# Sigmoids, scan and exponentials of the decay placed one to two chunks later in the orders of ACT and VectorE of a recurrent layer

## The chip, the cores and the metric

One core of a Trainium2 chip runs one program. The metric is device time in microseconds (us) for one execution. TensorE is called PE, its weight load PEld, VectorE DVE, ScalarE ACT, GpSimd POOL and SyncE SP, as in the profile.

## What is computed

One inference step of a two-layer decoder trunk on a prompt of 512 tokens and 8 x 8 sampled tokens (576 columns in all), model width 1024, in 32-bit floats. Layer 0 mixes tokens by windowed attention, layer 1 by RWKV-7 time mixing; each is followed by a dense SwiGLU block, and every sub-layer ends in a layer norm. The part that matters here is the time mixing, in the reference's words cut to the decay and the state:

```python
w = -jax.nn.softplus(-(w0 + jnp.tanh(xw @ w1) @ w2)) - 0.5
a = jax.nn.sigmoid(a0 + (xa @ a1) @ a2)
kk = heads(k * k_k)
kk = kk / jnp.maximum(jnp.sqrt(jnp.sum(kk * kk, axis=-1, keepdims=True)), 1e-12)
decay = jnp.exp(-jnp.exp(heads(w)))
...
sa = jnp.einsum('bhvk,bhk->bhv', S, -kk_t)
S = (S * d_t[:, :, None, :] + sa[..., None] * (kk_t * a_t)[:, :, None, :]
     + v_t[..., None] * k_t[:, :, None, :])
```

The kernel uses that the logarithm of the decay is a constant times a sigmoid. It sums these logarithms along the tokens of a chunk with a scan, and takes exponentials of the sums.

## The kernel before, in words

The layout has features on the 128 partitions and tokens along the free axis. A dense product (helper `slab`, L657) splits both operands into a high and a low part and multiplies three times; these products, in all projections and in both SwiGLU blocks, fill most of the time and come before and after the stretch of interest.

**The recurrent layer** works on *units*. Unit 0 holds the sampled tokens of all heads; units 1 to 8 are the eight pairs of heads for the prompt (512 tokens, one pair on the 128 partitions). The prompt is cut into 8 *chunks* of 64 tokens. The loop over `SLOTS` = 12 *slots* overlaps several units. In slot s these run together:

- A1, unit i = s (slots 0 to 8): sigmoids, decay, normed keys, and the scaled operands for the unit.
- A2, unit a = s - 1: the inverse of a small triangular matrix, level by level (`level_y`, `level_x`), token-major copies of b, k and v, and the masked Gram matrices.
- SB, sampled pair j = s - 2, and C, the group norm and gate of pair g = s - 4.
- B, pair q = s - 3 (slots 3 to 10): the state chain over the 8 chunks, the only part that is serial over chunks.

The state chain of one chunk c goes: PE `chain_u` (L1012, L1016), DVE copies the result into `uc` (L2074), PE `chain_sa` (L1026), ACT copies into `sac` (L1600), PE `chain_s` (L1037), DVE updates the state `S_c` (L2082, L2085). The next chunk starts from `S_c`. ACT also scales the last state into `spc` (L1593) ahead of each chunk.

**What sets the order.** Each engine has a list written out by hand: `for s in range(SLOTS)`, `for c in range(NCH)`, and in each chunk c branches that put the other work of the slot between the links of the chain. The three lists are in `slot` for PE, in ACT's loop at L1667 and in DVE's loop at L2141. POOL has a plain list for each slot: the level masks, the sample masks, the scaled gate (L588), the scaled r (L594), then the scaled keys (L609). SP moves the sampled state in and out. Semaphores carry every dependence between the lists.

**The functions that the edit places.**

- `sigmoids(i)` on ACT waits for `lora2(i)` of PE (L860 and L861, in chunk 0 after `chain_s`), then writes the sigmoid of the decay's logits into `cc` (L1501) and the sigmoid for a into `sga` (L1504). In slots 1 to 8 it is preceded by a load of ACT's function table.
- `cumulated(i)` on DVE waits for the first of these and runs the scan over `cc` in place (L1993).
- `decays(i)` on ACT asks for the other function table (L1515), waits for the scan, and writes two exponentials (L1521 into `e2`, L1522 into `e0`).

Their readers: `kk_sum` on PE (L873, chunk 2 after `chain_s`) waits for the first sigmoid; `kk_floor` on DVE (L2000, chunk 2) follows it; `kk_root` on ACT (a logarithm L1530 and an exponential L1532) stands in chunk 3 ahead of `chain_sa`; `scaled_z` on DVE (chunk 4) reads `e0`; POOL's scaled gate and scaled r read `e2` and `e0`, and `scaled_b` (chunk 5) and `bonus_terms` (chunk 7) on DVE read what POOL wrote. `dev_squares(g)`, a square of 512 columns (L1640), stands in ACT's chunk 2.

In the kernel before, ACT runs `sigmoids` in chunk 0 after its token-major copy of b, and `decays` in chunk 1 after the copy of k. DVE runs `cumulated` at the end of chunk 0, after the state update `chain_s` and so ahead of the `uc` copy of chunk 1.

Of the kernel before, what the change touches and what calls it, by code (L numbers as in the profile page):

```python
# [137 lines left out]
def build_program(nc, ins, outs, scratch):  # L138
    cols, width = constant_layout()
    ctx = ExitStack()  # L140
    with ctx:
# [137 lines left out]
        def psb(b):  # L279

            return ps[:, b, :]
# [1004 lines left out]
        def _(act):  # L1286
# [209 lines left out]
            def sigmoids(i):  # L1496

                act.wait_ge(ev("wkv_zero"), 1)
                act.wait_ge(ev("lora2_mm"), i + 1)
                if i:  # L1500
                    A(padded[:, :, 1:], chunks(psb(G1)), ACT.Sigmoid, bias=col(R_W0, i - 1)).then_inc(ev("sig_w"), 1)  # L1501
                    act.wait_ge(ev("ga"), i)
                    act.wait_ge(ev("f"), i)
                    A(sga[:], psb(G2), ACT.Sigmoid, bias=col(R_A0, i - 1)).then_inc(ev("sig_a"), 1)  # L1504
                    return
                for j in range(NPAIR):
                    out = A(padded_s[:, j, :, 1:], ps[:, G1, tk(j)].rearrange("p (b t) -> p b t", t=DT), ACT.Sigmoid, bias=col(R_W0, j))
                out.then_inc(ev("sig_w"), 1)
                for j in range(NPAIR):
                    out = A(sga[:, tk(j)], ps[:, G2, tk(j)], ACT.Sigmoid, bias=col(R_A0, j))  # L1510
                out.then_inc(ev("sig_a"), 1)

            def decays(i):

                nc.scalar.preload_act_table_set("natural_log_exp_and_others")  # L1515
                act.wait_ge(ev("scan"), i + 1)
                if i:
                    act.wait_ge(ev("kt"), i)
                    act.wait_ge(ev("zt"), i)
                    act.wait_ge(ev("rt"), i)  # L1520
                    A(chunks(e2[:]), padded[:, :, 1:], ACT.Exp, scale=KAPPA).then_inc(ev("e2"), 1)  # L1521
                    A(e0[:, 0:PADP], cc[:], ACT.Exp, scale=-KAPPA).then_inc(ev("e0"), 1)  # L1522
                else:
                    A(sequences(e2[:]), padded_s[:, :, :, 1:], ACT.Exp, scale=KAPPA).then_inc(ev("e2"), 1)
                    A(e0[:], cc_s[:], ACT.Exp, scale=-KAPPA).then_inc(ev("e0"), 1)
# [141 lines left out]
            for s in range(SLOTS):  # L1667
                i, a, j, q, g = s, s - 1, s - 2, s - 3, s - 4
                A1, A2, SB, B, C = i < UNITS, 0 <= a < UNITS, 0 <= j < NPAIR, 0 <= q < NPAIR, 0 <= g < NPAIR
                CSM = s == SLOTS - 2  # L1670
                whole = A2 and a >= 1
                if C:
                    last_state(g)
                    outputs(g)
                if A1:
                    kk_squares(i)
                for c in range(NCH):
                    if B and c >= 1:
                        scaled_state(q, c)
                    if c == 0 and whole:  # L1680
                        corner(a)
                    elif c == 1 and A2:
                        level_y(a, 1)
                    elif c == 2:
                        if C:
                            dev_squares(g)
                        if CSM:
                            dev_squares_s()
                    elif c == 3 and A1:
                        kk_root(i)  # L1690
                    elif c == 4 and SB:
                        sample_state(j)
                    elif c == 5 and whole:
                        level_y(a, 4)
                    elif c == 6 and A1:
                        key_mix(i)
                    elif c == 7:
                        if whole:
                            merge_t(a)
                    if B:  # L1700
                        chain_sa(q, c)
                    if c == 0:
                        if A2:
                            token_major(a, 0, "tb", "tok_b")
                        if A1:
                            sigmoids(i)
                    elif c == 1:
                        if A2:
                            token_major(a, 1, "tkk", "tok_k")
                        if A1:  # L1710
                            decays(i)
                    elif c == 2 and A2:
                        level_y(a, 2)
                    elif c == 3:
                        if A2:
                            token_major(a, 2, "tv", "tok_v")
                        if whole:
                            level_y(a, 3)
                        if CSM:
                            gn_root_s()  # L1720
                    elif c == 4 and C:
                        gn_root(g)
                    elif c == 5 and A1:
                        chunk_decays(i)
                    elif c == 6:
                        if SB:
                            sample_sa(j)
                        if whole:
                            merge_y(a)
                    elif c == 7:  # L1730
                        if A2:
                            inverse_blocks(a)
                        if C:
                            operand_high(g)
                        if SB:
                            sample_update(j)
                        if CSM:
                            act.wait_ge(ev("normed_step"), normed_at("z_s"))
                            A(zh[:, :, SEQ:T], chunks(outs_s[:]), ACT.Copy).then_inc(ev("normed_step"), 1)
# [23 lines left out]
        def _(dve):  # L1763
# [377 lines left out]
            for s in range(SLOTS):  # L2141
                i, a, j, q, g = s, s - 1, s - 2, s - 3, s - 4
                A1, A2, SB, B, C = i < UNITS, 0 <= a < UNITS, 0 <= j < NPAIR, 0 <= q < NPAIR, 0 <= g < NPAIR
                CSM = s == SLOTS - 2
                whole = A2 and a >= 1
                for c in range(NCH):
                    if B:
                        chain_u(q, c)
                    if c == 0 and A2:
                        level_first(a)  # L2150
                    elif c == 3 and A2:
                        level_x(a, 2)
                    elif c == 4:
                        if A1:
                            scaled_z(i)
                        if whole:
                            level_x(a, 3)
                        if CSM:
                            hat_s()
                    elif c == 5:  # L2160
                        if A1:
                            scaled_b(i)
                        if SB:
                            sample_ut(j)
                        if C:
                            bonus(g)
                        if CSM:
                            bonus_s()
                    elif c == 6:
                        if SB:  # L2170
                            sample_u(j)
                        if A1:
                            mixed_keys(i)
                    elif c == 7:
                        if SB:
                            sample_out(j)
                        if A1:
                            bonus_terms(i)
                    if B:
                        chain_s(q, c)  # L2180
                    if c == 0 and A1:
                        cumulated(i)
                    elif c == 1 and A2:
                        level_x(a, 1)
                    elif c == 2 and A1:
                        kk_floor(i)
                    elif c == 3 and A1:
                        unit_keys(i)
                    elif c == 4 and C:
                        hat(g)  # L2190
                    elif c == 5 and whole:
                        level_x(a, 4)
                    elif c == 6:
                        if C:
                            gated(g)
                        if A2:
                            masked_gram(a, 0, G1, "br", "incl")
                    elif c == 7:
                        if A2:
                            masked_gram(a, 2, G2, "kz", "strict")  # L2200
                            masked_gram(a, 1, G1, "kr", "incl")
                        if CSM:
                            gated_s()
# [39 lines left out]
```

## Time and profile before

| what | value |
|---|---|
| median of 3 runs | 2028.53 us (2024.49 to 2029.5) |
| profiled execution, its own time | 2028.29 us |
| span of the profiled execution, first to last instruction | 2026.5 us |
| PE busy | 1748.2 us (86%), 20270 matmuls |
| DVE, ACT, POOL busy | 679.6, 683.4, 613.4 us |
| mean granted PE clock | 0.914 of full speed |
| slots 3 to 8, from the first `uc` copy of slot 3 | 1106.3 to 1380.4 us |
| slot 9 | 1380.4 to 1422.9 us |

How to read it: "busy" counts the time in which an engine executed instructions; matmuls are pipelined, so their busy time is modelled. Times of a timeline are us from the start of the span. A row of the timeline has the start, the duration, the engine, the line of the kernel, the operation, output<-inputs, the shape and how many instructions were merged; in brackets is the idle time of the engine just before, and who ended it. A row of a group has the line, the engine, the count, then busy us and mean ns of one, then the idle time before and what ended it. In a row of busy times by stretch stand the stretch, its length, the busy time of PE, PEld, DVE, ACT and POOL with the number of their instructions, the mean granted clock of PE (1.00 is full speed), the share of the DMA engines and GB/s. "issue" is time in which an engine waited for nothing that the profile shows. The chunks of a slot are told apart by the `uc` copies of DVE (L2074), one in each.

### The profile page before, as it was taken

The page shows a single profiled execution, that of the slowest core. Times are in us where ns is not written, and L with a number is a line of the kernel's source. Part 1 is how long each engine was busy: PE and PEld are TensorE (multiplying, and loading weights), DVE is VectorE, ACT ScalarE, POOL GpSimd, SP SyncE. Part 2 cuts the span into 40 slices and gives each one's busy share as a digit, 9 for nine tenths or more (in the row PEclk, how much of TensorE's full clock was granted, in tenths as well). Part 3 has the DMA queues.
Part 4 walks back from the last instruction along what each step waited for, and adds up shares of the span by engine and source line. Part 5 has one row for each costly group of instructions (what it writes and reads, how often), then busy time and mean ns, then how long its engine had stood idle before and what let it go on. Part 6 is the DMA issues. An engine that isn't in the chain of part 4 may idle for free.

```text
span 2026.5 us, 46453 instructions
## 1 busy us (share of the span) xinstructions
PE 1748.2 (86%) x20270; PEld 1578.7 (78%) x20270; DVE 679.6 (34%) x942; ACT 683.4 (34%) x1118; POOL 613.4 (30%) x316
## 2 busy tenths in 40 slices
PE   4989696999998993888967888888885999998994
PEld 4965495999998993877936766666575999998994
DVE  2136246222222226233034344443246222222224
ACT  3135214433331112232235454443234433332112
POOL 3313123433333332222214222221033333333331
PEclk8969787999999997899978899999788999999997
DMA  7410012222222221312110000000041222222221
GB/s 214 113 36 1 21 52 70 84 83 83 83 83 75 82 82 66 105 46 72 42 24 14 14 15 15 15 15 10 12 126 42 80 79 81 82 83 82 85 71 47
DMA packets 236247, 125.93 MB, mean 62 GB/s; under 512 B 49275, under 2 KB 233196, under 8 KB 235956
## 3 DMA queue, kind: packets, MB, share of 16 engines
q1 hardware_dynamic: 227330, 108.97, 19.2%
q10 hardware_dynamic: 8786, 14.98, 2.3%
q8 instruction: 110, 1.80, 0.4%
q14 instruction: 21, 0.17, 0.0%
HBM read 116.33 MB, written 12.64 MB: 64 GB/s over the span
## 4 chain that ended last, share of the span: by engine, by line
PE 69%; issue 15%; DVE 8%; POOL 4%; ACT 3%; ACTq 1%; POOLq 0%; DVEq 0%
PE ps L657 51%; POOL wl L522 2%; PE ps L751 1%; PE ps L946 1%; PE ps L827 1%; PE ps L936 1%; PE ps L1026 1%; PE ps L776 1%; DVE xl L1968 1%; DVE x L1817 1%; PE ps L1037 1%; POOL x L537 1%; DVE mf L1962 1%; PE ps L915 1%; PE ps L1016 1%
## 5 line engine op out<-in xcount | busy, mean ns | idle before, releaser
L522 POOL TENSOR_TENSOR wl<-raw,wh 128x1024 fp32r<-128x1024 f32 (+1 forms) x172 | 451.3, 2625 | 878.2 <-ACT wh L1294 878.2
L657 PE MATMUL ps<-xh,wh 128*128 128x288 f32 x2112 | 460.8, 300 | 92.2 <-DVE xl L1968 40.0
L1294 ACT CAST wh<-raw 128x1024 fp32r<-128x1024 f32 (+1 forms) x172 | 190.3, 1108 | 843.4 <-PE ps L657 843.4
L657 PE MATMUL ps<-xl,wh 128*128 128x288 f32 x2112 | 457.4, 299 | 0.0
L657 PE MATMUL ps<-xh,wl 128*128 128x288 f32 x2112 | 456.8, 298 | 0.0
L657 PEld LDWEIGHTS ps<-xh,wh 128*128 128x128 f32 x2112 | 344.7, 191 | 99.1 <-issue 82.2
L657 PEld LDWEIGHTS ps<-xl,wh 128*128 128x128 f32 x2112 | 345.8, 192 | 0.0
L657 PEld LDWEIGHTS ps<-xh,wl 128*128 128x128 f32 x2112 | 345.3, 191 | 0.0
L1843 DVE TENSOR_TENSOR lnw<-lnw,ps 128x576 f32<-128x576 f32 x44 | 33.2, 754 | 390.2 <-PE ps L657 373.1
L657 PE MATMUL ps<-hh,wh 128*128 128x288 f32 x704 | 151.4, 297 | 11.3 <-DVE hl L1848 11.3
L657 PE MATMUL ps<-hl,wh 128*128 128x288 f32 x704 | 151.0, 296 | 0.0
L657 PE MATMUL ps<-hh,wl 128*128 128x288 f32 x704 | 150.9, 296 | 0.0
L657 PEld LDWEIGHTS ps<-hh,wh 128*128 128x128 f32 x704 | 114.3, 191 | 11.7 <-POOL wl L522 11.7
L657 PEld LDWEIGHTS ps<-hl,wh 128*128 128x128 f32 x704 | 114.2, 190 | 0.0
L657 PEld LDWEIGHTS ps<-hh,wl 128*128 128x128 f32 x704 | 114.0, 190 | 0.0
L1848 DVE TENSOR_TENSOR hl<-lnw,hh 128x576 f32 x44 | 97.0, 2205 | 46.2 <-ACT hh L1338 46.2
L1789 DVE TENSOR_TENSOR x<-x,ps 128x576 f32 x32 | 24.1, 755 | 256.5 <-PE ps L657 256.5
L1794 DVE TENSOR_TENSOR lnw<-lnw 128x576 f32<-128x576 f32 x32 | 80.6, 2520 | 3.9 <-ACT lnw L1321 3.5
L603 POOL TENSOR_TENSOR zl<-oS,zh 128x512 fp32r<-128x512 f32 x8 | 10.1, 1267 | 205.7 <-ACT zh L1652 205.7
L1956 DVE SCALAR_TENSOR_TENSOR mt<-xx,prm,x 128x576 f32<-128x576 f32 x24 | 23.7, 992 | 98.0 <-PE ps L657 97.3
L827 PE MATMUL ps<-mf,lnw 128*64 128x288 f32 (+2 forms) x128 | 42.3, 467 | 14.7 <-DVE mf L1962 14.4
L2085 DVE SCALAR_TENSOR_TENSOR S_c<-ps,pc,spc 128x64 f32<-128x64 f32 x56 | 15.6, 279 | 106.5 <-PE ps L1037 104.5
(340 smaller groups left out, 2320.8 us busy)
## 6 DMA issues: line engine op xcount, KB each, us to landing
raw<-in_ffn_w_gu SPq DMA_DIRECT2D x88, 512.0 KB, 3.8
raw<-in_ffn_w_down SPq DMA_DIRECT2D x32, 704.0 KB, 4.6
raw<-in_rwkv_w_rkv SPq DMA_DIRECT2D x24, 512.0 KB, 4.1
raw<-in_attn_w_qkv SPq DMA_DIRECT2D x24, 256.0 KB, 3.7
raw<-in_attn_w_o SPq DMA_DIRECT2D x32, 128.0 KB, 3.0
raw<-in_rwkv_w_o SPq DMA_DIRECT2D x8, 512.0 KB, 4.3
spread<-table ACTq DMA_DIRECT2D x1, 3072.0 KB, 15.5
x_kept<-x ACTq DMA_DIRECT2D x1, 2304.0 KB, 8.2
```

The source lines that it names most:

```text
L522: nc.gpsimd.tensor_tensor(wl[:, s, 0:ph.kb, :], raw[:, s, 0:ph.kb, :], wh[:, s, 0:ph.kb, :].bitcast(F32), ALU.subtract).then_inc(raw_free, 1)
L537: nc.gpsimd.tensor_tensor(x[:, j, :], x[:, j, :], lnw[:, 0, :], ALU.subtract).then_inc(ev("ln_sub"), 1)
L657: out = mm(ps[:, 2 * a + b, 0:TH], w[:, s, k, :], o[:, k0 + k, t0:t0 + TH], start=(first and k == 0 and w is wh and o is high), stop=(last ...
L751: out = mm(ps[:, 2 * (t % 2) + i // 2, (i % 2) * W:(i % 2 + 1) * W], qkvT[part, G * GROUP + i, qb * WIN:(qb + 1) * WIN], qkvT[part, KB + G ...
L776: out = mm(ps[part, 6 + pair % 2, :], vtok[:, qb - nkb + 1 + kb, g * HD:(g + 1) * HD], PT[:, u % 2, kb * 512:(kb + 1) * 512], start=(kb == ...
L827: out = mm(ps[part, bank + b, 0:TH], w(k), mf[:, k % 2, t0:t0 + TH], start=(k == 0), stop=(k == KB - 1))
L1294: nc.scalar.copy(wh[:, s, 0:ph.kb, :], raw[:, s, 0:ph.kb, :]).then_inc(hi_done, 1)
L1789: V.tensor_tensor(blk, blk, acc(a), ALU.add).then_inc(acc_free, 1)
L1794: V.tensor_tensor(squares, squares, lnw[:, 3:4, :], ALU.add).then_inc(ev("ln_acc"), 1)
L1843: V.tensor_tensor(hbuf[:, q, :].rearrange("p (h n) -> p h n", h=2), gbuf[:, q, :].rearrange("p (h n) -> p h n", h=2), acc(2 * q + 1), ALU.mult
L1848: V.tensor_tensor(hl[:, bass.ds(2 * i + q, 1), :], hbuf[:, q:q + 1, :], hh[:, bass.ds(2 * i + q, 1), :].bitcast(F32), ALU.subtract).then_i ...
L1956: V.scalar_tensor_tensor(mt[:, j % 2, :], xx[:, j, :], col(R_MIX + operand[1], j), x[:, j, :], ALU.mult, ALU.add).then_inc(ev("mt"), 1)
```

## The change

It moves three calls in two lists. On ACT `sigmoids(i)` goes from chunk 0 to chunk 1, after the token-major copy of k, and `decays(i)` from chunk 1 to chunk 2, after `level_y(a, 2)`. On DVE `cumulated(i)` goes from the end of chunk 0 to chunk 2, between the `uc` copy and the state update. The lists of PE, POOL and SP, all operands and all semaphores stay.

```diff
                     if c == 0:
                         if A2:
                             token_major(a, 0, "tb", "tok_b")
-                        if A1:
-                            sigmoids(i)
                     elif c == 1:
                         if A2:
                             token_major(a, 1, "tkk", "tok_k")
                         if A1:
+                            sigmoids(i)
+                    elif c == 2:
+                        if A2:
+                            level_y(a, 2)
+                        if A1:
                             decays(i)
-                    elif c == 2 and A2:
-                        level_y(a, 2)
...
                     if c == 0 and A2:
                         level_first(a)
+                    elif c == 2 and A1:
+                        cumulated(i)
                     elif c == 3 and A2:
...
                     if B:
                         chain_s(q, c)
-                    if c == 0 and A1:
-                        cumulated(i)
-                    elif c == 1 and A2:
+                    if c == 1 and A2:
                         level_x(a, 1)
```

## Rows read from the trace of the kernel before

**Rows 1.** The page, part 4: the chain that ended last, by engine, share of the span.

```profile
PE 69%; issue 15%; DVE 8%; POOL 4%; ACT 3%; ACTq 1%; POOLq 0%; DVEq 0%
```

**Rows 2.** Busy us: slots 3-8, 7, 9, chunk 1: PE, PEld, DVE, ACT, POOL, PEclk.

```profile
1106.30:1380.40 274.10, 234.44 (x7535) 183.16 (x7536) 113.44 (x266) 132.98 (x306) 68.16 (x65) 0.93 0.08 16
...
1290.80:1335.40 44.60, 38.53 (x1268) 29.53 (x1270) 19.26 (x46) 22.68 (x53) 12.03 (x11) 0.96 0.08 16
...
1380.40:1422.90 42.50, 36.98 (x1251) 28.43 (x1250) 14.14 (x38) 15.37 (x42) 7.47 (x8) 0.96 0.05 11
...
1298.70:1303.60 4.90, 4.67 (x130) 4.25 (x130) 1.23 (x5) 2.42 (x4) 0.89 (x1) 0.68 0.02 3
```

**Rows 3.** Groups by line in slots 3 to 8.

```profile
L1026 PE MATMUL ps<-uc,tt 64*64 64x64 f32 x192 | 17.0, 255 | 19.8 <-DVE uc L2074 19.1 <-issue 0.2
...
L915 PE MATMUL ps<-cst,kx 64*64 64x64 f32 x192 | 11.2, 305 | 0.0
...
L1993 DVE TENSOR_TENSOR_SCAN cc<-reset,cc 128x520 f32<-128x520 f32 x6 | 8.8, 1465 | 19.9 <-ACT cc L1501 19.9
...
L1501 ACT ACT_TABLE_LOAD x6 | 7.7, 1283 | 9.8 <-PE ps L861 9.8
...
L873 PE MATMUL ps<-sq,cst 128*128 128x512 f32 x12 | 6.8, 645 | 0.0
...
L861 PE MATMUL ps<-twa,wa 64*128 64x512 f32 x12 | 6.7, 641 | 0.0
```

**Rows 4.** Timeline of slot 7, chunk 0 to the copy of chunk 1.

```profile
1290.80 0.23 DVE L2074 COPY uc<-ps 128x64 f32<-128x64 f32 x1 [1.05 <-PE ps L1012]
...
1295.15 0.33 PE L1016 MATMUL ps<-S_c,zr 64*64 64x64 f32 x4
...
1295.31 1.28 ACT L1501 ACT_TABLE_LOAD   x1 [1.40 <-PE ps L861]
...
1297.19 0.68 ACT L1504 ACTIVATE sga<-ps,prm 128x512 f32<-128x512 f32 x1
...
1298.68 0.19 DVE L2074 COPY uc<-ps 128x64 f32<-128x64 f32 x1
```

**Rows 5.** Timeline of slot 9, chunk 1.

```profile
1384.05 0.33 PE L1016 MATMUL ps<-S_c,zr 64*64 64x64 f32 x4 [0.25 <-DVE S_c L2082]
...
1384.43 0.23 DVE L2074 COPY uc<-ps 128x64 f32<-128x64 f32 x1 [0.43 <-PE ps L1016]
...
1386.54 0.60 ACT L1558 ACTIVATE tok<-ps 128x512 f32<-128x512 f32 x1 [0.82 <-PE ps L915]
...
1386.89 0.45 PE L946 MATMUL ps<-xt,yb 32*32 32x32 f32 x32
```

**Rows 6.** Timeline of slot 7, chunks 1 to 3.

```profile
1301.99 1.28 ACT L1515 ACT_TABLE_LOAD   x1
...
1302.00 0.75 PE L946 MATMUL ps<-xt,yb 32*32 32x32 f32 x64
...
1303.82 0.62 ACT L1522 ACTIVATE e<-cc 128x520 f32<-128x520 f32 x1
...
1305.06 0.21 ACT L1600 ACTIVATE sac<-ps 128x64 f32<-128x64 f32 x1
...
1305.29 0.38 ACT L1563 ACTIVATE yb<-ps 128x256 f32<-128x256 f32 x1
...
1307.82 0.63 ACT L1530 ACTIVATE sq<-sq 128x512 f32<-128x512 f32 x1 [1.45 <-DVE sq L2000]
...
1309.02 0.21 ACT L1600 ACTIVATE sac<-ps 128x64 f32<-128x64 f32 x1
```

**Rows 7.** PE in slot 9, chunk 3, and the instruction queue in slots 3 to 8.

```profile
1396.25 0.33 PE L1047 MATMUL ps<-gr,tok 64*64 64x64 f32 x3 [1.06 <-issue]
...
q8 instruction: 59, 0.97, 1.5%
```

**Rows 8.** Timeline of ACT in slot 1: the key norms' logarithm.

```profile
1066.66 0.63 ACT L1530 ACTIVATE sq<-sq 128x512 f32<-128x512 f32 x1 [1.23 <-DVE sq L2000]
```

## The prediction

> **What bounds the kernel now.** I read the page first: over the whole execution PE holds 69% of the chain that ended last and waiting without a shown cause ("issue") 15% [rows 1]. That average is mostly dense products, which the edit doesn't touch. The edit lies in the recurrent layer's slots, so I read busy time by stretch. Six slots (3 to 8) both run the state chain of one head pair (B) and start the next unit (A1): 274.1 us, 45.7 each, with PE busy 234.4 [rows 2]. Slot 9 runs the chain but starts no unit: 42.5 us.
>
> Inside a slot the chain alternates PE, DVE, PE, ACT, PE, DVE in each chunk, and each engine takes its list in order. So an instruction that waits on ACT or DVE holds up the chain link listed behind it. The groups of the six slots show where: the scan of the decays (L1993) left DVE idle 19.9 us before it, waiting for the sigmoid of ACT, and runs 1.465 us each; PE then sat 19.1 us for DVE's `uc` copy in front of L1026; ACT's table load before the sigmoid waited 9.8 us for L861 [rows 3]. That is 3.3 us of DVE waiting and about 2.7 us of PE idling once a slot. The timeline of slot 7 shows the order: the chain's next product L1016 is done by about 1295.5, yet its copy starts at 1298.68, because ACT first loads the table (1295.31), computes both sigmoids (until 1297.87), and DVE scans [rows 4]. Slot 9, without these, starts that copy 0.38 us after L1016 starts (1384.05 to 1384.43) [rows 5]. What limits chunk 0 is thus the ACT sigmoid plus the scan, and not PE.
>
> A second cost follows the idle. In the 4.90 us of chunk 1 of slot 7 the granted clock was 0.68 of full speed, the slot's mean is 0.96 [rows 2]: PE had idled and then ran partly at 1.2 instead of 2.4 GHz. The token transposes L915 took 11.2 us of PE in six slots, 305 ns a matmul [rows 3].
>
> **The change part by part.** No instruction is added or removed: the same two sigmoids, two table loads, two exponentials and one scan a slot, no DMA, and nothing moves in the lists of PE, POOL or SP. I work it out in slot 7. Times in us of the trace.
>
> 1. *Sigmoids and scan leave chunk 0.* DVE copies `uc` for chunk 1 at 1295.15 + 0.38 = 1295.53 instead of 1298.68: 3.15 earlier [rows 4, 5].
>
> 2. *Chunk 1 without the idle.* In slot 9 L946 starts 2.46 after the `uc` copy (1384.43 to 1386.89) [rows 5]; in slot 7 it takes 3.32 (1298.68 to 1302.00) [rows 4, 6]. I take slot 9's: another 0.86, so L946 at 1297.99, 4.0 earlier. Bounds: 0 if PE stays at the low level, 0.86 if it doesn't; I take the latter, since the idle that comes before the low clock is what goes.
>
> 3. *Sigmoids in chunk 1.* ACT evicts the token-major keys at +2.11 after the copy (1386.54) for 0.60, so it is free at 1298.24 [rows 5]. The block of load and two sigmoids is 1295.31 to 1297.87, 2.56 [rows 4], and ends at 1300.80. Today the end of the exponentials (1304.44) is followed by `sac` of chunk 2 at 1305.06, 0.62 later [rows 6]; so `sac` comes at 1301.42. That is 3.64 earlier: 0.36 of the gain is given back, the rest of the block runs beside PE's and DVE's level step and `uc` copy. The scan, now set between chunk 2's `uc` copy and its L2085 in DVE's list, starts at about 1300.25, when the first sigmoid is done, and with 1.465 [rows 3] ends at 1301.7. L2085 needs `sac`, which ends at 1301.64, and a PE product after it, so the scan is just covered.
>
> 4. *Exponentials in chunk 2.* After `sac` ACT copies one level (1305.29, 0.38) [rows 6]; by the same offsets it is free at 1302.03. Load and two exponentials are 1301.99 to 1304.44, 2.45, and end at 1304.48. The root's logarithm L1530 could start at `sac` + 2.76 = 1304.18 (1305.06 to 1307.82 today) and waits until about 1304.7, past one small copy; with the 1.20 from it to the next `sac` [rows 6] this `sac` is at 1305.9, against 1309.02: 3.1 earlier. From there on the lists are as before.
>
> 5. *Who waits for the exponentials.* POOL's scaled gate and scaled r start when they are done and are read by DVE only in chunks 5 and 7; DVE's scaled z, in chunk 4, is the first reader of all. The exponentials end in chunk 2, so one chunk (4.9 us in slot 7 [rows 2]) or more covers them; were that cover gone, up to 2.45 a slot would show.
>
> A rule speaks against steps 3 and 4. Slot 7's load starts at 1301.99 and its last exponential ends 2.45 later, the load itself being 1283 ns in all the slots [rows 3, 6]. The Trainium skill (ScalarE: Activation LUTs, "What ACT_TABLE_LOAD costs") adds a drain of about 1380 ns to each load, some 2.66 us for a switch. By that each moved block would be 1.38 longer and a slot would gain about 0.3 us, an estimate by that page; the trace shows no room for the drain, and I go by the trace.
>
> 6. *Slots 1 and 2* have no state chain; there the key norms depend on ACT. ACT idles 1.23 before the logarithm [rows 8]; a block of 2.45 set before it can cost 0 to 1.2 in each. I take 0.5: 1.0 together. Slot 0 runs one unit alone, in the same dependence order: nothing.
>
> 7. *What comes late next: PE's instructions.* A denser PE shows stalls that waiting hid. In slot 9 PE stood 1.06 in the middle of L1047, cause "issue", and the six slots fetched 59 packets, 0.97 MB, of instructions [rows 7]. Bounds per slot: 0, and 1.06. Stalls in chunks 1 and 2 fall under the ACT blocks; for chunk 3 on I take half, 0.5.
>
> The Trainium skill (Runtime: NRT & Kernel Launch, "Instruction fetch mechanics") says that instructions come in blocks of 16 KiB and that the cost is mostly hidden. By that item 7 would be nothing, and the time would be 2010.7, an estimate by that page.
>
> Sum: 6 x (3.1 - 0.5) = 15.6, less 1.0, is 14.6 us. The profiled execution took 2028.29 us (1.8 more than its span), 0.2 under the median of the runs, 2028.53, so the sum needs no correction: 2028.3 - 14.6 = 2013.7.
>
> **The rivals.** About 0.3% (6 us) is what a measurement of this kernel can tell from no change.
>
> *A, as summed* (0.72): 11 to 21 us faster. 21 is six times 3.5, with no stall and a little more of the low clock gone.
>
> *B, PE's own supply is the bound* (0.16). For it: slot 9, free of all that moves here, still took 42.5, and the matmuls that it lacks are L873, 1.1 us of PE a slot (6.8 in six), and the pair L860 and L861, which overlap, 1.1 more (6.7) [rows 3]; with them it would take 44.7, against 45.7 on average [rows 2]. Against it: slot 9's stalls beyond slot 7's lie partly where ACT now sets the pace. It gives 6 x 1.0 = 6 us: 2022.3, at the edge of what can be told.
>
> *C, the blocks are given back in full, slower* (0.05). Place: ACT between `sac` of chunk 1 and `sac` of chunk 3. If neither block finds time in which ACT idles, the chain pays 2.56 + 2.45 = 5.0 a slot against the 4.0 won in chunks 0 and 1; with slots 1 and 2 at their 1.2 each that is 6 x 1.0 + 2.4 = 8.4 slower: 2036.7. It decides once more than 4.0 of the 5.0 shows. Against it: ACT is busy only 2.42 of the 4.90 us of chunk 1 [rows 2].
>
> *D, chunk 0 isn't freed* (0.05). The PE link L1016 stands behind L861 and the copy behind it; if PE, not the scan, set that copy, nothing would move: 2028 or so. Against it: L1016 starts 3.5 before the copy [rows 4].
>
> *E, more than 21 us* (0.02), by the low clock vanishing from other chunks too.
>
> The range is A's with half of B's reach: 2007.5 to 2021.5. Faster by over 0.3% is A, E and two thirds of B, 0.84; within 0.3% the rest of B and D, 0.11; slower C, 0.05.
>
> **What would show it.** Right: the wait of L1993 falls from 19.9 to under 3 us over the slots, the one of L1026 from 19.1 to a few; the `uc` copy of chunk 1 comes 4.7 us after that of chunk 0 instead of 7.9; L915 nears 218 ns as other transposes; slots of about 43; the seconds before `sac` in chunks 2 and 3 go to ACT. Wrong: equal gaps from chunk 0 to 1, PE stalls by "issue" growing by 2 us a slot (B), a wait of L2085 for the scan or of PE for `sac` of chunk 3 by over 2 us (C), or a time that changes in the dense products, where nothing was edited.

## The result and the profile after

The changed kernel took 2008.25 us (median of 4 runs, 2000.65 to 2011.49) beside 2029.01 us for the kernel before (median of 4, 2024.49 to 2035.79). The ratio is 0.989, 95% interval 0.9848 to 0.9931. On the prediction's base of 2028.53 us that is 2028.53 x 0.989 = 2006.2 us, just under the low end of the range (2007.5), where 2013.7 was forecast. The direction was right, the gain half as large again as forecast. A second, longer measurement of the same file gave 2009.34 against 2027.71 us, 0.9906 [0.9874, 0.9938]; on the same base that is 2009.5 us, inside the range. So the size of the miss is between 4 and 6 us, and the stretches below say where it lies.

The page of the kernel after: its span and instruction count, busy times, and the chain that ended last by engine (part 4).

```profile
span 1998.9 us, 46453 instructions
...
PE 1729.4 (87%) x20270; PEld 1565.8 (78%) x20270; DVE 679.6 (34%) x942; ACT 682.3 (34%) x1118; POOL 610.1 (31%) x316
...
PE 68%; issue 15%; DVE 8%; ACT 4%; POOL 4%; ACTq 1%; POOLq 0%; DVEq 0%
```

It hardly differs from [rows 1]: the edit is too small to be seen in averages. The stretches show it. Here are slots 3 to 8, slot 7, and chunk 1 of slot 7, in the columns of [rows 2] (length, then busy us of PE, PEld, DVE, ACT, POOL, the granted clock, DMA share, GB/s).

```profile
1102.20:1353.80 251.60, 223.71 (x7535) 172.86 (x7535) 112.64 (x266) 131.18 (x306) 65.44 (x65) 0.99 0.08 17
1270.00:1312.40 42.40, 37.91 (x1266) 28.54 (x1269) 19.12 (x45) 22.54 (x53) 11.11 (x11) 1.00 0.09 18
1274.80:1279.40 4.60, 4.27 (x196) 3.67 (x194) 1.28 (x5) 2.98 (x6) 3.11 (x4) 1.00 0.04 9
```

The six slots went from 274.1 to 251.6 us, and two things make up the 22.5. PE's busy time fell by 10.7 us (234.4 to 223.7) with the same matmuls, since the mean clock rose from 0.93 to 0.99. PE's idle time fell by 11.8 (39.7 to 27.9). The difference of the two profiled executions, 2028.29 - 2000.65 = 27.6 us, is larger than either median says. Of it 7.2 lie in the attention stage (from its first matmul, L730, to its last, L810: 145.2 to 138.0 us), where nothing was edited; over the fourteen profiles of this study that stage took 138.0 to 145.5. So slots are compared with slots here, and whole times only by medians.

The groups of slots 3 to 8, in the columns of [rows 3]: busy, mean ns of one | idle before, releaser.

```profile
L1026 PE MATMUL ps<-uc,tt 64*64 64x64 f32 x192 | 15.9, 243 | 3.6 <-DVE uc L2075 3.2
L1501 ACT ACT_TABLE_LOAD x6 | 7.7, 1283 | 0.1
L1994 DVE TENSOR_TENSOR_SCAN cc<-reset,cc 128x520 f32<-128x520 f32 x6 | 7.4, 1241 | 2.2 <-ACT cc L1501 2.2
L915 PE MATMUL ps<-cst,kx 64*64 64x64 f32 x192 | 6.8, 218 | 0.2 <-issue 0.2
```

PE's wait for the `uc` copy fell from 19.1 to 3.2 us, the scan's wait for the sigmoid from 19.9 to 2.2, the sigmoid's load now starts without a wait, and L915 runs at 218 ns instead of 305. The scan itself takes 1.24 us instead of 1.47. The timeline of slot 7, which answers to [rows 4] and [rows 6]:

```profile
1274.39 0.33 PE L1016 MATMUL ps<-S_c,zr 64*64 64x64 f32 x4
...
1274.77 0.23 DVE L2075 COPY uc<-ps 128x64 f32<-128x64 f32 x1 [1.17 <-PE ps L1016]
...
1277.50 1.28 ACT L1501 ACT_TABLE_LOAD   x1
...
1279.38 0.68 ACT L1504 ACTIVATE sga<-ps,prm 128x512 f32<-128x512 f32 x1
...
1279.51 1.24 DVE L1994 TENSOR_TENSOR_SCAN cc<-reset,cc 128x520 f32<-128x520 f32 x1
...
1280.66 0.23 ACT L1600 ACTIVATE sac<-ps 128x64 f32<-128x64 f32 x1
...
1281.56 0.32 PE L936 MATMUL ps<-xs,lm 32*32 32x32 f32 x14 [0.66 <-issue]
...
1281.94 0.38 ACT L1563 ACTIVATE yb<-ps 128x256 f32<-128x256 f32 x1 [1.04 <-PE ps L936]
...
1282.34 1.28 ACT L1515 ACT_TABLE_LOAD   x1
...
1284.17 0.62 ACT L1522 ACTIVATE e<-cc 128x520 f32<-128x520 f32 x1
...
1284.94 0.61 ACT L1530 ACTIVATE sq<-sq 128x512 f32<-128x512 f32 x1
...
1286.12 0.20 ACT L1600 ACTIVATE sac<-ps 128x64 f32<-128x64 f32 x1
```

Slot 7 begins at 1270.04, so the copy of chunk 1 (1274.77) comes 4.73 us into the slot; it was 7.88 [rows 4]. The copy starts 0.38 after L1016, as in slot 9. The scan now runs between the `uc` copy and the state update of chunk 2, and each `sac` follows the ACT block set before it. The level step L936 stops for 0.66 us in the middle, and ACT's next copy (L1563) waits for it.

### The profile page after: what moved, and what is told of

Its sections match the earlier page's. It is cut to its first block, busy times and chain, and to the rows that moved or that the text cites. A ratio compares the mean times of both kernels' runs of the same rounds, so it can differ in the third digit from the quotient of the medians.

```text
span 1998.9 us, 46453 instructions
## 1 busy us (share of the span) xinstructions
PE 1729.4 (87%) x20270; PEld 1565.8 (78%) x20270; DVE 679.6 (34%) x942; ACT 682.3 (34%) x1118; POOL 610.1 (31%) x316
## 4 chain that ended last, share of the span: by engine, by line
PE 68%; issue 15%; DVE 8%; ACT 4%; POOL 4%; ACTq 1%; POOLq 0%; DVEq 0%
PE ps L657 52%; POOL wl L522 3%; PE ps L936 1%; PE ps L827 1%; PE ps L946 1%; DVE xl L1969 1%; PE ps L1026 1%; DVE x L1818 1%; PE ps L776 1%; ACT S L1403 1%; POOL x L537 1%; DVE mf L1963 1%; PE ps L751 1%; PE ps L1037 1%; DVE S L1892 1%
## 5 line engine op out<-in xcount | busy, mean ns | idle before, releaser
L537 POOL TENSOR_TENSOR x<-x,lnw 128x576 f32<-128x576 f32 x16 | 30.3, 1924 | 63.6 <-DVE lnw L1811 63.6
```

Of the source, the lines that this page charges most:

```text
L537: nc.gpsimd.tensor_tensor(x[:, j, :], x[:, j, :], lnw[:, 0, :], ALU.subtract).then_inc(ev("ln_sub"), 1)
```

## The experiments

The theory T is the prediction's mechanism, resized after the result: the scan and what it waits for keep the `uc` copy of chunk 1 back by 3.15 us a slot; that idle time of PE brings the low clock behind it; both go. The rivals of each run are in its expectation. The table is the yardstick: length of slots 3 to 8 (from `uc` copy to `uc` copy), mean length of chunks 0 to 3 in them and the sum of chunks 4 to 7, then the us that PE ran at the lower clock level (1.2 GHz) by the trace's clock records, PE's "issue" waits with their count, and PE busy, all within those slots. For the fourteen profiles, in us:

| kernel | slots 3-8 | c0 | c1 | c2 | c3 | c4-7 | low clock | issue | PE busy |
|---|---|---|---|---|---|---|---|---|---|
| before | 274.0 | 8.39 | 5.10 | 4.23 | 3.64 | 24.31 | 41.0 | 6.6, 10 | 234.3 |
| before again (e9) | 273.1 | 8.40 | 5.02 | 3.96 | 3.81 | 24.32 | 34.1 | 8.5, 13 | 232.3 |
| after | 251.6 | 5.22 | 4.26 | 4.55 | 4.09 | 23.83 | 6.8 | 8.9, 15 | 223.7 |
| after again (e1) | 252.0 | 5.20 | 4.33 | 4.58 | 3.92 | 23.98 | 6.8 | 9.1, 15 | 223.9 |
| e2 scan only | 254.5 | 5.28 | 5.25 | 4.03 | 3.87 | 23.98 | 3.4 | 11.1, 15 | 221.1 |
| e3 blocks in chunk 1 | 267.5 | 5.23 | 4.24 | 7.41 | 3.90 | 23.83 | 27.3 | 6.7, 10 | 229.1 |
| e4 exponentials only | 271.3 | 8.39 | 4.46 | 4.34 | 4.02 | 24.02 | 30.7 | 6.1, 10 | 230.6 |
| e5 late from slot 3 | 252.8 | 5.20 | 4.59 | 4.50 | 4.07 | 23.76 | 3.4 | 10.6, 17 | 222.9 |
| e6 idle put back | 279.5 | 9.41 | 5.06 | 4.45 | 3.98 | 23.68 | 37.5 | 6.2, 9 | 233.0 |
| e7 blocks left out | 254.9 | 5.19 | 4.51 | 4.20 | 3.82 | 24.77 | 17.1 | 12.1, 15 | 226.0 |
| e8 root behind link | 257.0 | 5.21 | 4.59 | 4.63 | 3.71 | 24.69 | 13.7 | 14.2, 19 | 225.0 |
| e10 smaller idle | 253.6 | 6.71 | 3.68 | 4.40 | 3.81 | 23.67 | 6.8 | 5.4, 8 | 222.1 |
| e11 stream +128 | 257.6 | 4.75 | 4.54 | 4.65 | 4.09 | 24.91 | 23.9 | 9.9, 17 | 229.8 |
| e12 stream +64 | 259.9 | 5.73 | 4.57 | 4.55 | 4.12 | 24.37 | 17.1 | 13.4, 20 | 228.1 |

### e1: the changed kernel again

No edit.

> The changed kernel once more, with five rounds. The theory (T) has three parts: the scan's wait ahead of the uc copy was 3.1 us in each of slots 3 to 8, PE's low clock after that idle cost 0.9 more in chunk 1 and about as much again in other chunks, and the two ACT blocks give back 0.8 a slot; slots 0 to 2 lose 2.9. By T the six slots again take 251 to 254 us (before: 274.1) and the time falls by 18 to 23 us. Rival L (luck of the profiled run): the low clock outside chunk 1 comes back, the six slots take 256 to 260 us, and the time falls by 14 to 17 us.

Measured 2009.34 us, 0.9906 [0.9874, 0.9938]. The windows row of slots 3 to 8:

```profile
1106.30:1358.30 252.00, 223.87 (x7536) 172.38 (x7538) 112.59 (x266) 131.17 (x306) 65.42 (x65) 0.99 0.08 17
```

Both figures of T hold (251 to 254 us, 18 to 23 us less). The six slots repeat within 0.4 us, so their gain is no accident of one profile.

### e9: the kernel before again

No edit; one run, 2034.34 us.

> The kernel before once more, for a second profile of it. T: chunk 0 takes 7.9 to 8.9 us in all six slots, L915 about 300 ns a matmul, slots 3 to 8 take 270 to 275 us. Of the first profile's 6.0 us for chunk 6 of slot 3, where others have 3.9, T says nothing; if it is 3.9 here, 2 us of the profiled gain of slots 3 to 8 are chance. Rival: the six slots repeat at 274 within 0.5 us and all of the 22.4 us gained belong to the change.

```profile
1108.60:1381.70 273.10, 232.26 (x7531) 181.65 (x7533) 113.15 (x266) 132.72 (x306) 68.18 (x65) 0.94 0.08 16
```

The slots repeat within 1 us, as T asks; so does the 6.0 us of chunk 6 of slot 3. Slots 0 to 2 do not: 72.13 us here, 69.45 in the first profile of the same file. That matters for e5.

### e2: only the scan moves

```diff
+                    elif c == 1 and A1:
+                        cumulated(i)
...
-                    if c == 0 and A1:
-                        cumulated(i)
-                    elif c == 1 and A2:
+                    if c == 1 and A2:
```

Against the kernel before. ACT's list stays as it was, with sigmoids in chunk 0 and exponentials in chunk 1.

> Of the three moves only the scan is moved, to chunk 1 of DVE behind the uc copy; sigmoids and exponentials stay in chunks 0 and 1. T: the uc copy of chunk 1 comes 4.7 us after that of chunk 0, as in the changed kernel, sac of chunk 1 waits about 1 us for the sigmoids, and nothing stands in chunk 2, so that a slot gains 2.8 us plus the clock, against 3.1 plus the clock: six slots 252 to 257 us, slots 0 to 2 at their old length, time 15 to 21 us less. Rival S (the sigmoids' place is what counts, since ACT serves the chain): the chain only moves its wait from DVE to ACT and the six slots take 264 us or more.

Measured 2013.42 us, 0.991 [0.9877, 0.9944], 14.3 less than before where T wanted 15 to 21; the slots are inside T's 252 to 257. Two groups of slots 3 to 8, and PE's wait for `sac` there (sum, count, longest):

```profile
L1993 DVE TENSOR_TENSOR_SCAN cc<-reset,cc 128x520 f32<-128x520 f32 x6 | 8.4, 1393 | 9.4 <-ACT cc L1501 9.4
L915 PE MATMUL ps<-cst,kx 64*64 64x64 f32 x192 | 6.8, 218 | 0.2 <-issue 0.2
```

```profile
PE ps L1037 <- ACT sac L1600: 6.7, 12, 1.0
```

The scan alone brings the slots to 254.5, 19.1 us under the mean of the two profiles of before (273.6), of the 21.8 that the whole change brings (to 251.8). The low clock is gone. What the moved ACT blocks add is in chunk 1: 5.25 against 4.3, since the `sac` of chunk 1 behind the sigmoids is late by up to 1.0 us; of the 1.0 us a slot, chunk 2 gives 0.5 back and chunk 3 0.1.

### e4: only the exponentials move

```diff
+                    elif c == 2:
+                        if A2:
+                            level_y(a, 2)
                         if A1:
                             decays(i)
-                    elif c == 2 and A2:
-                        level_y(a, 2)
```

Against the kernel before: the exponentials go to chunk 2, the sigmoids and the scan stay. The sigmoids alone were not moved in any run.

> Of the three moves only the exponentials are moved, to chunk 2; sigmoids and scan stay in chunk 0. T: chunk 0 keeps its 7.9 to 8.9 us, sac of chunk 2 comes 0.6 earlier and the logarithm of chunk 3 waits for the block, so a slot changes by less than 0.5 us: six slots 272 to 277 us, time within 0.3% of before. Rival: the exponentials' block in chunk 1 was a cost by itself; without it the six slots fall below 270 us.

Measured 2029.91 us, 1.0 [0.9979, 1.0022]; PE's wait for `uc` in slots 3 to 8:

```profile
PE ps L1026 <- DVE uc L2075: 19.2, 12, 3.0
```

The wait is the old one (19.1). Chunk 1 is shorter by 0.6, chunks 2 and 3 longer by 0.54 together. The six slots took 271.3 us, 2.3 under before and 0.7 under T's range; 2.1 of that is chunk 6 of slot 3, which took 3.89 us here and 6.01 in both profiles of before. By itself this move is worth nothing that can be measured.

### e3: both blocks in chunk 1

```diff
                             sigmoids(i)
-                    elif c == 2:
-                        if A2:
-                            level_y(a, 2)
-                        if A1:
                             decays(i)
+                    elif c == 2 and A2:
+                        level_y(a, 2)
```

Against the changed kernel: ACT's copy into `sac` for chunk 2 now stands behind both blocks.

> The changed kernel with the exponentials back in chunk 1, right behind the sigmoids; the scan stays in chunk 2. T: both ACT blocks and the scan between them stand ahead of sac of chunk 2, which comes 2.2 us later than in the changed kernel; nothing stands in chunk 2 after it (0.5 back): a slot is 1.6 us longer, six slots 260 to 263 us, time 9 to 13 us less than before. Rival S2 (ACT blocks are covered wherever they stand): as the changed kernel, 251 to 254 us.

Measured 2022.05 us, 0.9977 [0.9955, 0.9999], 5.7 less than before where T gave 9 to 13. PE's wait for `sac` in slots 3 to 8, and slot 7's timeline:

```profile
PE ps L1037 <- ACT sac L1600: 16.4, 11, 2.9
```

```profile
1291.51 0.62 ACT L1522 ACTIVATE e<-cc 128x520 f32<-128x520 f32 x1
...
1293.02 0.48 PE L1037 MATMUL ps<-sac,tok 64*64 64x64 f32 x4 [2.28 <-ACT sac L1600]
...
1294.06 2.07 PE L873 MATMUL ps<-sq,cst 128*128 128x512 f32 x2
```

PE stands 2.28 us for `sac`, and what follows runs at the lower clock level (granted 0.50 from 1293.0 to 1296.4): L873 takes 2.07 for its two matmuls where six such pairs took 6.8 before [rows 3], 1.13 each. ACT never waited for the scan; it went from block to block without a pause, so it is the length of the two blocks that keeps `sac` back. Chunk 2 grows by 2.8 us, and 15.7 of the 21.8 us are gone (251.8 to 267.5), more than the 8 to 11 that T gave it. T had counted the wait and not the clock behind it. So the place of the exponentials does matter, if the sigmoids are moved too: it is both blocks ahead of one `sac` that cost.

### e6 and e10: idle time put back

```diff
-                    if c == 1 and A2:
+                    if c == 0 and A1 and B:
+                        for _ in range(6):
+                            link(V.tensor_tensor(l0[:], l0[:], l0[:], ALU.max))
+                    elif c == 1 and A2:
```

Against the changed kernel: DVE does six (e10: three) extra operations of no effect (the larger of a tile and itself) where the scan stood, so PE idles though ACT's order is the new one.

> The changed kernel with six short vector operations on a tile of DVE alone (about 2.8 us together) at the end of chunk 0 in slots 3 to 8: the idle of PE is back, and nothing else of the old order. T: a slot pays those 2.8 us, 0.9 for the low clock in chunk 1, L915 rises from 218 to about 300 ns a matmul, and low clock shows in other chunks too, so 3.5 to 4.5 us a slot: six slots 273 to 279 us, or as before. Rival F: the clock has no part in it and a slot pays 2.8 or less, six slots 268.5 us or less, L915 at 218 ns.

> As the run with the idle put back, with three of the six vector operations: they took 5.9 us together there, so about 2.9 here. T: chunk 0 is about 1.3 us longer than in the changed kernel (the operations begin at 5.0 us after the slot's first uc copy less 1.5, and the copy of chunk 1 could have come at 4.7), PE idles some 1 us, and the low clock doesn't return: six slots 258 to 262 us, low clock under 15 us, L915 near 218 ns. Rival: any idle in chunk 0 brings the low clock; L915 again near 290 ns and six slots over 263 us.

Measured 2038.78 us, 1.0061 [1.0037, 1.0086] for e6, and 2012.55, 0.9909 [0.9878, 0.994] for e10. The groups of e6, then of e10, in slots 3 to 8:

```profile
L2186 DVE TENSOR_TENSOR l<-l 128x256 f32<-128x256 f32 x36 | 33.2, 923 | 1.0
L1026 PE MATMUL ps<-uc,tt 64*64 64x64 f32 x192 | 16.9, 255 | 25.1 <-DVE uc L2075 24.6
L915 PE MATMUL ps<-cst,kx 64*64 64x64 f32 x192 | 10.5, 292 | 0.0
```

```profile
L2186 DVE TENSOR_TENSOR l<-l 128x256 f32<-128x256 f32 x18 | 17.9, 992 | 0.4
L1026 PE MATMUL ps<-uc,tt 64*64 64x64 f32 x192 | 15.8, 241 | 9.6 <-DVE uc L2075 9.1
L915 PE MATMUL ps<-cst,kx 64*64 64x64 f32 x192 | 6.6, 218 | 0.0
```

In e6 PE waits 24.6 us for the copy, about 4.1 a slot (21.8 of the 24.6 in chunk 1); L915 is back at 292 ns, PE's busy time at 233.0, and 37.5 us run at the low level. So idle time alone, with the scan and the sigmoids elsewhere, brings the low clock back. The operations took 923 ns, about twice what was set for them, so the wait overshot the old one and the slots with it: 279.5 us, 5.9 over before and 0.5 over T's 273 to 279. In e10 the wait is 9.1 us, 1.5 a slot, and the low clock stays away: 6.8 us, as without any wait. Here T failed: it wanted 258 to 262 us and 253.6 came. 1.5 us more in chunk 0 of each slot cost only 1.8 in all six instead of 6 to 10, as chunk 1 shrank by 0.6 to 3.68 and the later chunks by another 0.6 together. The last 1.5 us by which the copy comes earlier are worth little. That PE has work of its own list left at that point, done meanwhile in e10 and later otherwise, would explain it; no run takes that apart.

### e5: slots 0 to 2 in the old order

```diff
+                        if A1 and not B:
+                            sigmoids(i)
...
-                        if A1:
+                        if A1 and B:
...
-                    elif c == 2 and A1:
+                    elif c == 2 and A1 and B:
...
+                    if c == 0 and A1 and not B:
+                        cumulated(i)
```

Against the changed kernel (cut; the exponentials go likewise): the new places only where a state chain runs.

> The new places in the slots that run the state chain (3 to 8), the old places in slots 0 to 2. T: slots 0 to 2 return to their 69.4 us from kk_squares of unit 0 to the first uc copy (72.3 in the changed kernel), the six slots stay at 251 to 254; the time is 2 to 3 us under the changed kernel. Rival: the 2.9 us of slots 0 to 2 were the clock's chance, and their length stays within 1 us of 72.3.

Measured 2010.07 us, 0.9915 [0.9885, 0.9944]. Slots 0 to 2 took 69.63 us against 72.3 (after), as T asks. But e9 took 72.13 and e8, with the old order there too, 71.96. So the old order gave about 69.5 twice and about 72 twice; the five profiles with the changed kernel's order there (after, e1, e6, e7, e10) all lie between 72.0 and 72.4. The means differ by 1.3 us, the profiles of one order by 2.7, so a loss may be there, but neither its size nor the 2.9 us that T read from one pair of profiles is shown. The six slots stayed (252.8), and the time is no better than that of the changed kernel, where T wanted 2 to 3 us.

### e7: the blocks left out

```diff
+                if i >= 3:
+                    A(cc[:, 0:1], psb(G1)[:, 0:1], ACT.Copy).then_inc(ev("sig_w"), 1)
+                    ...
+                    A(sga[:, 0:1], psb(G2)[:, 0:1], ACT.Copy).then_inc(ev("sig_a"), 1)
+                    return
```

Against the changed kernel. From unit 3 on this leaves out the sigmoids of decay and a, the exponentials and their table loads, and puts one-column copies in their place.

> The changed kernel without the sigmoids of the decay and of a, the exponentials and the table loads in units 3 to 8 (copies of one column take their places); this part of the computation is left out. T: what the two blocks still cost in chunks 2 and 3 (0.8 us a slot) is gained, 4 to 6 us over the six slots, which take 246 to 248 us. Rival P (PE's supply of instructions is the bound): waits of PE with the cause issue grow as the others shrink, and the six slots stay at 250 us or more.

Measured 2009.1 us, 0.9907 [0.9876, 0.9939]: no better than with them. Some of PE's waits in slots 3 to 8, sum, count, longest:

```profile
PE ps L936 <- issue: 2.7, 4, 0.8
...
PE ps L1057 <- issue: 2.5, 3, 1.1
```

T wanted 246 to 248 us; 254.9 came. ACT's 25 us less busy time (131.2 to 105.7) shorten chunk 2 by 0.37 and chunk 3 by 0.2, and chunks 4 to 7 pay 0.9 for it, with "issue" waits of 12.1 us instead of 9, and 17.1 us of low clock, all of it in chunks 5 and 6. The kernel without these blocks is no faster, so what ACT still costs in the changed kernel isn't to be had by unloading ACT alone.

### e8: a wait less for `sac` of chunk 3

```diff
-                    elif c == 3 and A1:
+                    elif c == 3 and A1 and not B:
...
+                        if A1 and B:
+                            kk_root(i)
```

e5 with the logarithm of the key norms behind the `sac` of chunk 3 instead of before it (cut; DVE's use of it goes to chunk 4).

> As e5, and in slots 3 to 8 the key norms' logarithm and exponential come behind sac of chunk 3 instead of ahead of it, with the unit keys on DVE behind the uc copy of chunk 4. T: sac of chunk 3 comes up to 1.2 us earlier and no link waits instead, so a slot gains 0.5 to 1.2 us against e5: six slots 245 to 250 us. Rival: the unit keys and scaled z, now together in chunk 4, or PE's stalls take it back: six slots within 2 us of e5.

Measured 2015.44 us, 0.9924 [0.9897, 0.9951]. T missed again: it wanted 245 to 250 us for the six slots and 257.0 came, 4.2 over e5 and so beyond the rival's 2 as well. Chunk 3 went from 4.07 to 3.71, as planned, and chunks 4 to 7 from 23.76 to 24.69. Waits of PE in the slots:

```profile
PE ps L936 <- issue: 4.0, 5, 1.0
...
PE ps L946 <- issue: 2.8, 4, 1.3
...
PE ps L1057 <- issue: 2.1, 3, 1.0
```

Issue waits are at 14.2 us, the most of all runs, and the low clock at 13.7 (3.4 in e5). Two edits that take work or a wait off ACT both end in more issue waits and more low clock; which of the two costs the time isn't taken apart.

### e11 and e12: the instruction stream moved

```diff
+            for _ in range(256):
+                pe.wait_ge(ev("proj_taken"), 1)
             ident2 = const("ident2")
```

Against the changed kernel: waits on an event long passed, before the layer, shift all later instructions of PE in their stream. Two such waits make one instruction, so 256 of them are 128 instructions (e12: 128 waits, 64 instructions).

> The changed kernel with 128 more wait instructions in PE's list ahead of slot 0, each satisfied at once: every later instruction of PE lies 128 places further in its stream. Theory Q (PE's short stops with the cause issue sit where a block of the stream ends, so they move with the stream): inside slots 3 to 8 the stops are at other places, 1.4 to 2.2 us later or earlier in each slot, their sum is between 6 and 13 us, and the slots' length changes by up to 3 us either way. Rival: they belong to certain instructions and stay where they are in both profiles of the changed kernel (3.2 to 3.4 us into slot 4 at L906, 4.0 into slot 5 at L1041, about 11.3 into slots 7 and 8 at L936).

> As the one before with 64 instructions. Q: the stops move by about half as far, and the length of slots 3 to 8 lies anywhere within 3 us of 252. Rival: they stay.

In both profiles of the changed kernel PE stops in the middle of a group of matmuls mostly at the same places, for instance L906 in slot 4 (0.97 and 1.08 us) and L936 in slot 8 (0.93 and 0.89); some differ, as L936 in slot 3 (0.67 and 0.15). The first fence is slot 4 of the changed kernel; then the stop in front of L867, behind the waits, and one in slot 4 of e11; then one in slot 6 of e12.

```profile
1145.22 0.39 PE L906 MATMUL ps<-cst,bt 64*64 64x64 f32 x6 [0.97 <-issue]
```

```profile
1042.51 0.44 PE L867 MATMUL ps<-twa,wa 64*128 64x64 f32 x1 [15.45 <-issue]
...
1171.22 1.12 PE L875 MATMUL ps<-sq,cst 128*128 128x512 f32 x2 [1.56 <-issue]
```

```profile
1244.40 0.68 PE L908 MATMUL ps<-cst,bt 64*64 64x64 f32 x16 [2.06 <-issue]
```

The stops move with the stream, and the traces show what ends them. The DMA queue that brings instructions (q8) lands 59 packets in these six slots in every profile. Over the fourteen profiles PE has 193 issue waits there, and each of the 193 ends 1.18 to 1.71 us after such a packet has landed. That stretch behind the packets is about an eighth of the time, and of PE's 481 other waits about 7% end in it. So these stops are PE waiting for its own instructions and not for data. The six slots took 257.6 and 259.9 us, 6 to 8 more than before the shift, which was beyond the 3 us expected. PE's busy time rose by 6.0 and 4.3 us of this, with more low clock (23.9 and 17.1 us). The waits themselves cost much: slots 0 to 2 grew by 14.7 and 7 us, so the whole times say nothing of the shift, 2029.7 us, 1.0018 [0.9996, 1.004], and 2027.01, 0.9994 [0.9977, 1.001].

## Why the prediction was right or wrong

By its own steps, from means of two profiles each (before and e9; after and e1), per slot:

**Steps 1 and 2** were right. Chunk 0 fell by 3.18 us (3.15 forecast), chunk 1 by 0.77 (0.86). The copy comes 4.73 us into slot 7, as forecast. e2 shows that it is the scan's move that did it, and e6 that the low clock in chunk 1 comes from the idle time. e10 shows a limit: of the 3.15 us in chunk 0 the last 1.5 bring only 0.3 a slot.

**Steps 3 and 4** were right on the mean. Chunks 2 and 3 grew by 0.75 together, 0.9 forecast. In slot 7, where the working was done, `sac` of chunk 2 comes 10.62 us into the slot, as forecast, but `sac` of chunk 3 at 16.08 instead of 15.1, since the stop of 0.66 us in L936 keeps back ACT's copy and the block behind it. The wait for `sac` is 2.9 us in all and nowhere above 0.4:

```profile
PE ps L1037 <- ACT sac L1600: 2.9, 11, 0.4
```

The rule of the Trainium skill (ScalarE: Activation LUTs, "What ACT_TABLE_LOAD costs") on a drain for each load was rightly set aside: load, two activations and no gap between them, 1282.34 to 1284.79, again 2.45 us. e3 shows what keeps these steps cheap: both blocks before one `sac` cost 15.7 us.

**Step 5** was right that they cost nothing: DVE has no wait for the exponentials or for POOL in these slots, and e4 moves them at no measurable cost. POOL's wait for them did grow, by 5.3 us in six slots. The first line is before, the second after:

```profile
L588 POOL TENSOR_TENSOR ga<-sga,e 128x512 f32<-128x512 f32 x6 | 7.6, 1268 | 32.2 <-ACT e L1521 32.2
...
L588 POOL TENSOR_TENSOR ga<-sga,e 128x512 f32<-128x512 f32 x6 | 7.6, 1273 | 37.5 <-ACT e L1521 37.5
```

**Step 6** (1.0 us lost in slots 1 and 2) is neither shown nor refuted. Slots 0 to 2 took 1.3 us more in the mean of five profiles with the new order there than in that of four with the old, but they differ by 2.7 us between two profiles of the kernel before (69.45 and 72.13).

**Step 7, "What comes late next: PE's instructions", is the step that failed.** It allowed 0.5 us a slot, 3.0 us in six, for stalls in chunk 3 and later, and chunks 4 to 7 did not grow by 0.5: they fell by 0.41, 24.32 to 23.91. Issue waits did rise, from 7.6 to 9.0 us on the mean, but not where the step put them: in chunks 3 to 7 they fell, from 4.6 to 3.8 us in the six slots. The rise is in chunks 1 and 2, from nothing to 2.5 us, where the step had called them covered by the ACT blocks; in slot 7 the one of L936 was not. Among the waits after:

```profile
PE ps L936 <- issue: 3.4, 5, 0.9
...
PE ps L946 <- issue: 1.5, 3, 1.0
```

What the prediction saw in slot 9 (1.06 us) was a place in the stream and no rate that each slot pays (e11, e12).

The other part of the miss is rival E's mechanism, to which it gave 0.02: the low clock was not only in chunk 1. By the clock records of the two profiles of before, 23.8 and 20.4 us of it lay in chunk 1 of the six slots and 12.6 in chunks 5 and 6; after, none in chunk 1 and 6.5 and 6.8 in chunks 5 and 6. Chunk 6 of slot 3 is the plainest case. Here is its window in e9, then the same chunk after:

```profile
1140.50:1146.50 6.00, 5.88 (x126) 5.46 (x116) 2.02 (x6) 1.54 (x5) 0.00 (x0) 0.50 0.01 3
```

```profile
1133.70:1137.60 3.90, 3.83 (x100) 2.79 (x98) 1.61 (x4) 2.51 (x7) 1.27 (x1) 1.00 0.02 4
```

It took 6.0 us at 1.2 GHz in both profiles of before, and 3.9 and 4.2 in those of after, at 2.4 GHz for all or most of it. The sum per slot is then -3.18 - 0.77 + 0.75 - 0.41 = -3.6, six times that 21.7 us, where the forecast had -3.15 - 0.86 + 0.9 + 0.5 = -2.6 and 15.6. Of the missing 6 us, 5.4 are chunks 4 to 7 (0.9 x 6): 3.0 are the stalls that were forecast and didn't come, 2 are chunk 6 of slot 3. By the second measurement of the whole (18.4 us gained) the 3.0 alone are most of the miss.

What draws the low level in that chunk stays open, and with it whether the edit did it. It isn't the idle time of chunk 0: e6, with the fullest wait, has 4.1 us there and e4 3.9, while e7, without any, has 5.9. Order changes and a shift of the stream (e11 6.0, e12 3.9) both turn it on and off.

**The rivals.** B (PE's supply as the bound, a gain of 6 us) was wrong for this edit. Behind it something like B may hold: e7 and e8 take further work or waits off ACT and lengthen the six slots by 3.1 and 5.2 us, and the 1.5 us of waiting a slot in e10 cost only 1.8 in all. But the low clock rose along with the issue waits in e7 and e8, and chunk 6 of slot 3 alone, at 5.9 and 6.0 us, is 2 us of each. D fell with the `uc` copy at 4.73 us, C with chunks 2 and 3, which gave back 0.75 us a slot and not 5.0. The medians' difference of 20.8 us (18.4 in the second measurement) is at A's upper edge, which was E's border.

No variant clearly beats the changed kernel; e5 (2010.07) and e1 (2009.34) can't be told apart.

## What to carry to other kernels

When an engine's list holds a long operation that waits for another engine, look at what is listed behind it: moving only this scan past the chain's copy brought 19 of 22 us, and moving only the exponentials nothing that can be measured. Price the removal of a repeated idle time of PE with the granted clock behind it, over the whole stretch and not just the next chunk: here about half of the gain (10.7 of 22.5 us in the first pair of profiles, 9.5 of 21.8 by the means of two) is less busy time of PE on the same matmuls. And a stall seen once in an instruction stream has a place, so it isn't to be charged to each pass of a loop.

## What the runs showed of the hardware that was not expected

- PE's wait for `uc` of 3.2 us a slot (before, 19.1 in six) or 4.1 (e6) goes with 34 to 41 us of low clock in six slots; 1.5 a slot (e10) goes with 6.8, the same as 0.5 (after). So the low clock does not grow in proportion to the wait.
- PE waits for its own instructions 5.4 to 14.2 us in these six slots, up to 2.06 us at a time, mostly at places that stay the same from run to run and move when the stream is shifted. All 193 such waits of the fourteen profiles end 1.18 to 1.71 us after a packet of the instruction queue has landed, so this can be read from one trace. The Trainium skill (Runtime: NRT & Kernel Launch, "Instruction fetch mechanics") calls that cost mostly hidden; in this stage it is 2 to 6% of the time (5.4 of 253.6 us to 14.2 of 257.0).
- Waits already satisfied cost PE time: the 128 instructions of e11 made slots 0 to 2 longer by 14.7 us, the 64 of e12 by 7.0. Both give about 0.11 us an instruction.
- One and the same elementwise maximum of 128x256 on DVE took 424 to 426 ns in the seven cases of e6 in which POOL did nothing meanwhile, and 507 to 1149 ns in the 29 in which POOL was working for part or all of it (752 to 1149 in e10, where POOL always was).
